# Two batches of the first modulation at a time, from batch 12 on

## The chip, the cores and the metric

The kernel runs on one core of one Trainium2 chip. The metric is the device time of one execution in microseconds, as the median of the runs shown. The engines are named as the profile names them: PE is TensorE's matmul side, PEld its weight loads, DVE is VectorE, ACT is ScalarE, POOL is GpSimd and SP is SyncE, which here does nothing but issue loads and stores. "POOLq" and "SPq" are the two queues from which transfers are issued.

## What is computed

A two-layer backbone over 512 tokens and 256 context tokens, both 2048 wide, in float32. Only its start matters here:

```
shift, scale, gate       = split(silu(c) @ w_mod + b_mod, 3)        # w_mod: 2048 x 6144, layer 0
shift_c, scale_c, gate_c = split(silu(c_ctx) @ w_mod + b_mod, 3)
h  = rmsnorm(x,   g) * (1 + scale)   + shift       # 512 x 2048
hc = rmsnorm(ctx, g) * (1 + scale_c) + shift_c     # 256 x 2048
q, k, v, f, z = split(h @ w_in)                    # the first product made is k, and kc from hc
```

Windowed attention, a Fourier mixing, an output projection, a second layer with pooling and a last norm follow. The second layer's modulation and the gate of the first are made on DVE beside the later stages.

## The kernel before

All large products are made in three parts of reduced precision (high by high, high by low, low by high), so a value is first split into a high and a low part: ACT makes the high part (`w_hi`, `h_hi`, `hc_hi`), DVE the low one (`w_lo`, `h_lo`, `hc_lo`). A "unit" is one pair of 128-row tiles of the contraction, 0.5 MB of weights; a projection stage for 512 output columns has 8 units (HALVES), each used by 4 products of output tiles, m = 0 to 3.

The opening stage interleaves two things on PE, in an order written out by hand:

- The first modulation, in 32 batches (BATCHES). Batch k reads two loads of 0.5 MB of `w_mod`, 1 MB together, and issues 16 products with the conditioning vector as the stationary operand (the trace counts each product as two instructions). Batches 4p to 4p+3 add up to shift and scale of the pair of tiles p. After its last product a batch raises `mod_used`.
- The key projection of tokens and of context. A **key chunk** is one unit by one output tile over 512 tokens, 6 matmuls of 512 columns; a **context chunk** is the same over 256 context tokens. There are 32 of each. Chunks 4u to 4u+3 belong to unit u and need the normed, split pair u, which needs batches 4u to 4u+3.

`KEY_STEPS` and `CONTEXT_STEPS` say which chunks follow which batch: at step k PE runs `modulate(k)`, then the step's key chunks, then its context chunks; steps 32 and 33 have no batch. `opening_steps(start, counts, steady, total)` turns a list of counts from step `start` on, and `steady` after it, into ranges; step 32 is always filled up to chunk 27 and step 33 holds the last four.

The queues around it:

- **SP** loads the batches. There are three slots (BATCH_SLOTS) of 1 MB: two in `raw`, one in `modchunk`. `load_batch(k)` (L358) waits until batch k-3 is used. After batch 31, SP loads weights of the next stage into the same slots (L352).
- **POOL** issues the key weights one unit at a time into the single buffer `key_raw`: unit u+1 is issued (L396) when DVE has made the low part of unit u. Behind unit 7 it issues `cond_row` (1 MB), `rope` (0.5 MB) and `edges` (L401 to L403), which the stages after the opening need.
- **ACT** makes for each pair u the high part of the key weights (`hi(G_K, u)`, L437), which waits until PE has finished the context chunks of unit u-2, and after it the high parts of `h` and `hc` (L461).
- **DVE** turns the modulation of pair u (L953 to L958, once batch 4u+3 is used), norms the two tiles (L863), makes `w_lo` (L798), then `h_lo` (L872), then the context pair.

After the opening comes the value stage: its first unit (`w_lo` from `raw`) is split on ACT and DVE behind pair 7 and behind the conditioning row (L520, L996). From there on the stages are paced by PE.

Of the kernel before, what the change touches and what calls it, by code (L numbers as in the profile page):

```python
# [29 lines left out]
GROUP = 4  # L30
QUADRANT = P // 4
COLS = GROUP * P
HALVES = KT // 2
# [107 lines left out]
def opening_steps(start, counts, steady, total):  # L141

    at, steps = 0, []
    for k in range(BATCHES + 2):
        n = counts[k - start] if 0 <= k - start < len(counts) else steady * (k >= start)
        end = {BATCHES: total - GROUP, BATCHES + 1: total}.get(k, at + n)
        steps.append(range(at, end))
        at = end
    return steps


KEY_STEPS = opening_steps(3, (2, 1, 1, 0, 0, 1, 1, 1, 1, 0, 1, 1, 1, 1, 0, 1, 1, 1, 1, 1, 1, 0), 1, GROUP * HALVES)
CONTEXT_STEPS = opening_steps(7, (4, 0, 0, 2, 2, 0, 0, 0, 0), 1, GROUP * HALVES)
SUM_X_STEP, SUM_C_STEP = 1, 5
AWAKE_STEP, AWAKE_PRODUCTS = 3, 5
CONTEXT_SLOTS = 4
# [19 lines left out]
def build(nc, mod0, weights, modb, cond_in, xT, ctxT, vectors, wf, ident_in, identb_in, masks_in, rope_in, dft_tok_in,  # L176
          dft_ch_in, edges_in, outT):
    with ExitStack() as whole:
# [1204 lines left out]
        def _(pe):  # L1383
# [121 lines left out]
            pe.wait_ge(cond_ready, 1)  # L1505
            for k, (key_part, context_part) in enumerate(zip(KEY_STEPS, CONTEXT_STEPS)):
                if k < BATCHES:
# [367 lines left out]
```

## Time and profile before

| | us |
|---|---|
| median of 3 runs | 1447.12 |
| lowest and highest | 1446.72, 1449.27 |
| the profiled execution | 1448.78 |
| its span, first to last instruction | 1447.1 |
| PE busy in it | 1413.7 (98%) |
| DVE, ACT, POOL busy | 904.9, 501.2, 77.1 |
| PE in the chain that ended last | 88% |

Times in the trace are counted from the span's start. A duration of a matmul is longer than the distance to the next one, since matmuls overlap; for PE the distance between starts is what counts. The opening takes the first 137 us of the span.

### The profile page before, as it was taken

The page shows a single profiled execution, that of the slowest core. Times are in us where ns is not written, and L with a number is a line of the kernel's source. Part 1 is how long each engine was busy: PE and PEld are TensorE (multiplying, and loading weights), DVE is VectorE, ACT ScalarE, POOL GpSimd, SP SyncE. Part 2 cuts the span into 40 slices and gives each one's busy share as a digit, 9 for nine tenths or more (in the row PEclk, how much of TensorE's full clock was granted, in tenths as well). Part 3 has the DMA queues.
Part 4 walks back from the last instruction along what each step waited for, and adds up shares of the span by engine and source line. Part 5 has one row for each costly group of instructions (what it writes and reads, how often), then busy time and mean ns, then how long its engine had stood idle before and what let it go on. Part 6 is the DMA issues. An engine that isn't in the chain of part 4 may idle for free.

```text
span 1447.1 us, 20122 instructions
## 1 busy us (share of the span) xinstructions
PE 1413.7 (98%) x7714; PEld 1182.7 (82%) x7714; DVE 904.9 (63%) x1422; ACT 501.2 (35%) x730; POOL 77.1 (5%) x148
## 2 busy tenths in 40 slices
PE   5899999999999999999999999999999999999997
PEld 3688888888888888888888888888888888888897
DVE  6644555546767787776565676664555666674456
ACT  5223322234555443354222342121351323332233
POOL 0001111101100000000001101000000000010000
PEclk9999999999999999999999999999999999999998
DMA  9996567556711333324666666333233233366344
GB/s 385 379 378 248 175 204 251 176 174 201 230 58 58 103 117 116 111 78 145 203 191 196 195 190 190 117 101 102 88 102 98 92 97 93 93 203 187 105 144 172
DMA packets 65099, 236.87 MB, mean 164 GB/s; under 512 B 7232, under 2 KB 8128, under 8 KB 63744
## 3 DMA queue, kind: packets, MB, share of 16 engines
q1 hardware_dynamic: 43344, 157.83, 32.6%
q0 software_dynamic: 19712, 72.03, 15.7%
q10 hardware_dynamic: 1968, 5.95, 1.2%
q8 instruction: 54, 0.88, 0.3%
q14 instruction: 21, 0.17, 0.0%
HBM read 231.59 MB, written 4.19 MB: 163 GB/s over the span
## 4 chain that ended last, share of the span: by engine, by line
PE 88%; DMA 5%; DVE 5%; issue 1%; ACT 1%; SPq 0%; DVEq 0%; POOLq 0%; POOL 0%; ACTq 0%
PE ps L1385 86%; DMA modchunk<-in_modb 2%; DMA raw<-in_mod 2%; PE ps L1613 2%; DMA kvmem<-in_ctxT 1%; DVE modchunk L805 1%; DVE w_lo L798 1%; DVE stat L1065 0%; DVE pooled L1346 0%; DVE tmp L917 0%; DVE kvmem L981 0%; DVE pt_lo L1104 0%; DVE main L921 0%; ACT w_hi L437 0%; DVE tmp L1076 0%
## 5 line engine op out<-in xcount | busy, mean ns | idle before, releaser
L1385 PE MATMUL ps<-h_hi,w_hi 128*128 128x512 f32 (+1 forms) x1664 | 643.9, 387 | 2.7 <-DVE h_lo L872 1.3
L1385 PE MATMUL ps<-h_hi,w_lo 128*128 128x512 f32 (+1 forms) x1664 | 634.6, 381 | 0.0
L1385 PE MATMUL ps<-h_lo,w_hi 128*128 128x512 f32 (+1 forms) x1664 | 634.3, 381 | 0.0
L798 DVE TENSOR_TENSOR w_lo<-raw,w_hi 128x1024 fp32r<-128x1024 f32 x216 | 264.4, 1224 | 359.3 <-ACT w_hi L437 359.0
L437 ACT CAST w_hi<-raw 128x1024 fp32r<-128x1024 f32 x216 | 226.6, 1049 | 649.2 <-PE ps L1385 649.1
L1385 PEld LDWEIGHTS ps<-h_hi,w_hi 128*128 128x128 f32 x1664 | 312.9, 188 | 66.1 <-issue 7.7
L1385 PEld LDWEIGHTS ps<-h_hi,w_lo 128*128 128x128 f32 x1664 | 312.8, 188 | 61.3
L1385 PEld LDWEIGHTS ps<-h_lo,w_hi 128*128 128x128 f32 x1664 | 313.1, 188 | 57.0 <-issue 0.2
L805 DVE CUSTOM_DVE_ANT_0 modchunk<-modchunk,cond_row 128x1024 f32<-128x1024 f32 x128 | 154.7, 1220 | 20.3 <-DMA modchunk<-in_modb 20.1
L392 POOL DMA_DIRECT2D modchunk<-in_modb x128 | 67.6, 528 | 1143.3 <-DVE modacc L805 1117.5
L641 ACT CAST pt_hi<-ps 128x512 fp32r<-128x512 f32 (+1 forms) x48 | 30.7, 640 | 124.0 <-PE ps L1613 124.0
L1065 DVE TENSOR_REDUCE stat<-ps 128x1 f32<-128x513 f32 (+1 forms) x48 | 36.3, 757 | 38.2 <-PE ps L1385 38.2
L1244 DVE SCALAR_TENSOR_TENSOR ubuf<-raw,modv,ubuf 128x512 f32<-128x512 f32 x60 | 45.0, 749 | 2.3 <-DVE ubuf L1266 1.2
L1385 PE MATMUL ps<-raw,kvmem 128*32 128x128 f32 x704 | 26.1, 289 | 17.7 <-DMA raw<-in_mod 17.6
L1385 PEld LDWEIGHTS ps<-raw,kvmem 128*32 128x32 f32 x704 | 18.8, 114 | 23.6 <-issue 17.5
L1104 DVE TENSOR_TENSOR pt_lo<-ps,pt_hi 128x512 fp32r<-128x512 f32 (+1 forms) x48 | 36.1, 753 | 2.6 <-ACT pt_hi L641 2.4
L1385 PE MATMUL ps<-k_hi,q_hi 128*128 128x256 f32 (+1 forms) x96 | 32.5, 339 | 0.2 <-DVE q_lo L1046 0.2
L1385 PE MATMUL ps<-k_lo,q_hi 128*128 128x256 f32 (+1 forms) x96 | 28.4, 296 | 0.0
L1385 PE MATMUL ps<-k_hi,q_lo 128*128 128x256 f32 (+1 forms) x96 | 28.2, 294 | 0.0
L1385 PE MATMUL ps<-p_hi,w_hi 128*128 128x512 f32 x64 | 25.2, 394 | 0.0
L1385 PE MATMUL ps<-p_hi,w_lo 128*128 128x512 f32 x64 | 25.1, 392 | 0.0
L1385 PE MATMUL ps<-w_hi,h_lo 128*128 128x512 f32 x64 | 25.0, 390 | 0.0
(204 smaller groups left out, 1332.1 us busy)
## 6 DMA issues: line engine op xcount, KB each, us to landing
raw<-in_weights SPq DMA_DIRECT2D x216, 512.0 KB, 3.6
modchunk<-in_modb POOLq DMA_DIRECT2D x128, 512.0 KB, 4.6
raw<-in_mod SPq DMA_DIRECT2D x44, 512.0 KB, 6.8
modchunk<-in_mod SPq DMA_DIRECT2D x20, 512.0 KB, 6.9
main<-in_xT SPq DMA_DIRECT2D x4, 1024.0 KB, 8.3
main<-in_xT ACTq DMA_DIRECT2D x4, 1024.0 KB, 4.9
out<-pooled SPq DMA_DIRECT2D x14, 256.0 KB, 2.1
kvmem<-in_weights POOLq DMA_DIRECT2D x6, 512.0 KB, 7.1
```

The source lines that it names most:

```text
L392: pool.dma_start(modchunk[:, slot], src).then_inc(chunk_landed[slot], 16)
L437: nc.scalar.copy(w_hi[:, j % 2], src).then_inc(hi_ready, 1)
L641: nc.scalar.copy(*turned_tiles(k - 1, pt_hi)).then_inc(pt_hi_ready, 1)
L798: nc.vector.tensor_tensor(w_lo[:, j % 2], src, w_hi[:, j % 2].bitcast(F32), ALU.subtract).then_inc(lo_ready, 1)
L805: nc.vector.tensor_tensor_reduce(out=modchunk[:, half], in0=modchunk[:, half], in1=cond_row[:, half * (D // 2):(half + 1) * (D // 2)], sca ...
L1065: chain.link(nc.vector.tensor_reduce(stat[:, 0, par:par + 1], ps_flat[:, S_END - width:S_END], AX.X, ALU.max))
L1104: nc.vector.tensor_tensor(lo_part, turned_part, hi_part.bitcast(F32), ALU.subtract).then_inc(pt_ready, 1)
L1244: ins = nc.vector.scalar_tensor_tensor(out=bias_acc[g % 2], in0=raw[:, j % RAW_SLOTS, r], scalar=shift, in1=bias_acc[g % 2], op0=ALU.mult, ...
L1385: return nc.tensor.matmul(out, lhsT, rhs, start=start, stop=stop, skip_group_check=True)
L1613: ins = nc.tensor.transpose(ps_flat[:, 6 * 512 + t * P:6 * 512 + (t + 1) * P], probs[k % 2][:, t * P:(t + 1) * P], ident)
```

## The change

From batch 12 on PE takes two batches one after the other and then two key chunks and two context chunks, in place of one batch, one key chunk and one context chunk. The slots, the loads and what they wait for stay as they are.

```
-KEY_STEPS = opening_steps(3, (2, 1, 1, 0, 0, 1, 1, 1, 1, 0, 1, 1, 1, 1, 0, 1, 1, 1, 1, 1, 1, 0), 1, GROUP * HALVES)
-CONTEXT_STEPS = opening_steps(7, (4, 0, 0, 2, 2, 0, 0, 0, 0), 1, GROUP * HALVES)
+KEY_STEPS = opening_steps(3, (2, 1, 1, 0, 0, 1, 1, 1, 1) + (0, 2) * 10, 0, GROUP * HALVES)
+CONTEXT_STEPS = opening_steps(7, (4, 0, 0, 0, 2) + (0, 2) * 10, 0, GROUP * HALVES)
```

Worked out into chunks (key / context) after each batch:

| step | before | after |
|---|---|---|
| 10 | 1 / 2 | 1 / 0 |
| 11 | 1 / 2 | 1 / 2 |
| 12 | none | none |
| 13 | 1 / 0 | 2 / 2 |
| 14, 15 | 1 / 0, 1 / 0 | none, 2 / 2 |
| 16, 17 | 1 / 1, 0 / 1 | none, 2 / 2 |
| 18 to 23 | 1 / 1 each | none and 2 / 2 in turn |
| 24 | 0 / 1 | none |
| 25 | 1 / 1 | 2 / 2 |
| 26 to 31 | 1 / 1 each | none and 2 / 2 in turn |
| 32 | 3 / 4 | 0 / 2 |
| 33 | 4 / 4 | 4 / 4 |

Steps 0 to 9 are the same in both.

## Rows read from the trace of the kernel before

**Rows 1.** Windows: length, busy time (instructions) by engine, granted clock, DMA share, GB/s.
```profile
66.00:72.00 6.00, 4.16 (x71) 2.58 (x70) 3.66 (x8) 2.43 (x3) 0.10 (x1) 1.00 1.02 414
...
96.00:102.00 6.00, 6.00 (x93) 4.95 (x91) 4.66 (x9) 3.19 (x5) 0.53 (x1) 1.00 0.97 350
```

**Rows 2.** Waits of PE from 60 to 119.6: total us, times, longest.
```profile
PE ps L1385 <- DMA raw<-in_mod: 2.2, 4, 0.7
```

**Rows 3.** Chain that ended last: start us, length, what.
```profile
68.60 8.75 DMA raw<-in_mod
...
77.39 82.67 PE ps L1385 x784
```

**Rows 4.** Timeline of PE in the opening: start us, length, instruction, count, idle before.
```profile
54.58 0.28 PE L1385 MATMUL ps<-hc_hi,w_hi 128*128 128x256 f32 x1
...
60.10 1.96 PE L1385 MATMUL ps<-raw,kvmem 128*32 128x128 f32 x64
62.08 0.47 PE L1385 MATMUL ps<-h_hi,w_hi 128*128 128x512 f32 x1
...
74.48 1.08 PE L1385 MATMUL ps<-modchunk,kvmem 128*32 128x128 f32 x32
75.50 0.39 PE L1385 MATMUL ps<-hc_hi,w_hi 128*128 128x256 f32 x1
```

**Rows 5.** The same, around the last batches and up to the value stage.
```profile
117.70 0.28 PE L1385 MATMUL ps<-hc_hi,w_hi 128*128 128x256 f32 x1
...
118.50 1.08 PE L1385 MATMUL ps<-raw,kvmem 128*32 128x128 f32 x32
119.51 0.50 PE L1385 MATMUL ps<-h_hi,w_hi 128*128 128x512 f32 x1
...
121.00 0.28 PE L1385 MATMUL ps<-hc_hi,w_hi 128*128 128x256 f32 x1
...
121.71 0.39 PE L1385 MATMUL ps<-h_hi,w_hi 128*128 128x512 f32 x1
...
125.82 0.28 PE L1385 MATMUL ps<-hc_hi,w_hi 128*128 128x256 f32 x1
...
128.65 0.40 PE L1385 MATMUL ps<-h_hi,w_hi 128*128 128x512 f32 x1
...
136.95 0.40 PE L1385 MATMUL ps<-w_hi,h_hi 128*128 128x512 f32 x1
```

**Rows 6.** Batch loads issued 64.7-65.4 (batch 17), 99.7-100.4 (28), 109.7-110.4 (31), then 77.9-110.5.
```profile
L358 SPq DMA_DIRECT2D modchunk<-in_mod x2: 328/436/545, 64.8 to 65.1; - x2
DMA to landing us min/median/max: 8.1/8.5/9.0
...
DMA to landing us min/median/max: 7.5/7.9/8.3
...
DMA to landing us min/median/max: 5.1/5.9/6.6
...
DMA to landing us min/median/max: 4.2/6.2/8.3
```

**Rows 7.** Timeline of POOL from 111 to 113.5.
```profile
111.35 0.53 POOL L396 DMA_DIRECT2D kvmem<-in_weights  x1 [11.28 <-DVE w_lo L798]
111.86 0.53 POOL L401 DMA_DIRECT2D cond_row<-in_cond  x1
```

**Rows 8.** Timeline of DVE and of ACT: pair 3, then pair 7 and the first value unit.
```profile
68.23 0.32 DVE L953 STREAM_TRANSPOSE kvmem<-ps 128x128 f32<-128x128 f32 x1 [4.45 <-PE ps L1385]
...
71.52 1.41 DVE L872 SCALAR_TENSOR_TENSOR h_lo<-main,mod_v,h_hi 128x512 fp32r<-128x512 f32 x2
...
121.96 1.05 ACT L437 CAST w_hi<-kvmem 128x1024 fp32r<-128x1024 f32 x1 [8.25 <-PE ps L1385]
...
124.19 1.41 DVE L872 SCALAR_TENSOR_TENSOR h_lo<-main,mod_v,h_hi 128x512 fp32r<-128x512 f32 x2
...
132.84 1.22 DVE L798 TENSOR_TENSOR w_lo<-raw,w_hi 128x1024 fp32r<-128x1024 f32 x1
```

## The prediction

> **What bounds the kernel now.** I went from the whole to the part. In the chain that ended last PE has 88% and the one long piece that is not PE in this region ends at 77.4 us; from there the chain is PE's own work [rows 3]. So whatever shortens PE's sequence in the opening after 77.4 should move the end, if no wait takes its place. The waits of PE say what else is in the opening: from batch 12 on it waits 2.2 us in four places, each time for a batch's load [rows 2]. The windows explain why these waits stop: between 66 and 72 us the transfers run at 414 GB/s with PE at 4.16 of 6.00 us, so the loads set the pace; between 96 and 102 they run at 350 GB/s with PE busy throughout, so PE does, with some 15% of the transfer rate in hand [rows 1]. The granted clock is 1.00 in all of these windows, so no term of the sum comes from it.
>
> Then the distances between starts. A single batch takes 1.01 (118.50 to 119.51), the first key chunk behind it 1.49 (to 121.00), a context chunk behind that 0.71 (to 121.71), a key chunk behind a chunk 1.37 (three in 4.11, to 125.82), a context chunk in front of a batch 0.80 (117.70 starts the last one, 118.50 the batch) [rows 5]. Two batches in a row take 1.98 (60.10 to 62.08) [rows 4].
>
> **The change part by part.**
>
> *Fewer changes of kind.* Two steps of before cost 2 x (1.01 + 1.49 + 0.80) = 6.60. One pair of after costs 1.98 + 1.49 + 1.37 + 0.71 + 0.80 = 6.35. In steady steps that is 0.25 a pair; counted by kind, a change costs 0.12 (1.49 against 1.37) plus 0.09 (0.80 against 0.71) plus 0.04 (2.02 against 1.98), again 0.25. No product is added or dropped. From step 17 to 31 before has 15 groups of chunks behind a batch and after has 8: 7 x 0.25 = 1.75 us less. (Groups before step 17 don't count, since the loads set the pace there.)
>
> The Trainium skill ("TensorE: Matmul & The Clock Gate", Back-to-back issue gap) gives the distance of matmuls as set by the number of columns and the pipelined weight load, and knows no price for a change of kind. By that this term would be zero; the trace disagrees, with 1.49 against 1.37 for the same six products [rows 5].
>
> *Order up to batch 17.* Step 10 loses its two context chunks (1.4 us, from 54.58 on) [rows 4], so batch 13 ends between 60.7 and the 62.08 of now [rows 4], by how much of this its loads leave. Two groups of chunks at 4.37 and two pairs of batches at 1.98 later, at 73.4 to 74.8, batch 17 would be done by PE's own order. But the last half of its load is issued at 65.1 now and lands 9.0 later, at 74.1 [rows 6]; a rate that is full already won't bring it sooner. A batch needs half of its 1.01 after its second load, so batch 17 ends at 74.6, against 75.50 now [rows 4]: 0.9 gained. Bounds: 1.0, and nothing, since after issues this load two microseconds later than now (batch 14 waits for four chunks more), at about 67.2, and by the 8.3 of batch 28 it would land at 75.5.
>
> *What is behind it.* From 75.50 to the first chunk of unit 7 at 128.65 are 53.15 us [rows 4, 5]. Of these goes the last of the four waits (0.3, one of those in rows 2, the one that ends at 77.39 [rows 3]), the 1.75 for changes of kind, and one context chunk (0.71), which after has made by batch 17 (chunks 8 and 9 at step 15, where before had made chunk 8 alone by then). Remaining: 50.4. So unit 7 could start at 125.0 but for new waits: 3.65 gained.
>
> *New wait for loads.* With three slots batch k+3 is issued when batch k ends. The first batch of a pair then has nearly two pairs of time, the second has one: its second half is issued 0.5 after batch k and is wanted one pair, 6.35 us, after its own issue. Now it has three steps of 3.3 less a batch, 8.9. The latencies seen from 78 us on are 4.2 to 8.3, median 6.2 [rows 6]; so the cover is thin. But much of these is standing in line: in after nothing has been issued for 5.3 us when the second of a pair is, and the four loads of a pair take 4 x 1.27 = 5.1 at 414 GB/s [rows 1]. The line is empty, and I take the smallest latencies seen, 4.2, and 0.9 more for a second half, which is issued 0.4 behind the first and takes 1.27, so 5.1 [rows 6], plus 1.3 where POOL's key load of 0.5 MB shares the engines: 6.4 at most. No wait in the pairs 18/19 to 28/29; bounds 0 and 2.0, which is four pairs that meet a key load, each late by a quarter of the 2.0 by which batch 28's 8.3 would miss.
>
> Batch 31 is another matter. Its load goes out when batch 28 ends, at about 111.7. POOL issues the weights of unit 7 and behind them 1.5 MB for later stages when `w_lo` of unit 6 is made: at 111.35 and 111.86 now [rows 7], about 110.4 then. So 2 MB of POOL's and 1 MB of SP's are in flight together. If the two queues share evenly, batch 31 has its 4 halves' worth to wait for, two of its own and two of POOL's: 5.1 + 2 x 1.27 = 7.6, that is 1.3 late. Before, batch 31 with half of this overlap took 6.6 (0.3 late), and batch 28, issued right beside a key load, 8.3 (2.0 late) [rows 6]. I take 0.8; bounds 0 and 2.0.
>
> The Trainium skill ("DMA: Bandwidth & Descriptors", Queues, rings and completion order) says that each DMA engine takes turns between the queues it has work for, a packet at a time. By that rule it would be the even share, 1.3, and the result 0.5 worse than my sum; strict order of issue would give 3.0 or more. No row of before separates the two, since there the two queues overlap for a part of a batch only.
>
> *New wait for the splits.* Now unit 7's `h_lo` is made 6.1 us after batch 31 ends (119.51 to 125.6), because ACT's `w_hi` waits for PE's context chunks (idle 8.25 before it, until PE) [rows 8]. In after those chunks, of unit 5, are done two steps earlier, so the cast is off the chain, as for pair 3, where it took 68.1 to 72.93, 4.8 us [rows 8]. PE has between batch 31 and unit 7 two key and four context chunks: 1.49 + 1.37 + 4 x 0.71 = 5.7. So 5.7 against 4.8: no wait, 0.9 in hand. Were the cast still late, it would cost 0.4. The same holds for units 3 to 6 with 4.37 + 1.98 = 6.35 between.
>
> *The value stage.* It starts at 136.95, behind unit 7's 8.30 us, and its first `w_lo` is ready at 134.06 [rows 5, 8], 14.55 after batch 31 ended. The latter chain begins with pair 7, so it gets 1.1 shorter: 13.4 after batch 31, which ends at 74.6 + 7 x 6.35 + 0.8 = 119.85, thus 133.3. PE reaches unit 7 at 119.85 + 5.7 = 125.55 by this count, at 125.8 by the one above, and the value stage 8.3 later, at 133.85 to 134.1. Covered by at least 0.5; nothing lost. The loads of modb start when batch 31 is used, as before; the later stages are paced by PE, so the shift carries to the end.
>
> **Sum:** 0.9 + 0.3 + 1.75 + 0.7 - 0.8 = 2.85 us less. The profiled execution took 1448.78 with its span of 1447.1 us; it would become 1445.9. It lies 1.7 above the median of the runs, which is what is forecast: 1447.12 - 2.85 = 1444.3.
>
> **The rivals.**
>
> A. *The second batch of each pair is late* (slower). Place: PE in front of batches 19, 21 ... 29, with the slots full. Price: latency of a second half minus 6.35, in each of six pairs. It decides from 6.35 + 2.85/6 = 6.8 on; at the even-share 7.6 in all pairs it would cost 6 x 1.25 = 7.5, so 1444.3 + 7.5 = 1452. For it: the median of all latencies is already 6.2. Against: nothing else is in line when it is issued, and rates have room [rows 1]. Chance 0.09.
>
> B. *Late only beside POOL's key loads*, by the bound of 2.0 in all: 2.85 - 2.0 = 0.85 gained, 1446.3; if batch 31 is 2.0 late as well, 1447.5. For it the 8.3 of batch 28. Chance 0.27.
>
> C. *The change of kind costs the same somewhere else*, as the page has it: the 1.75 is not there: 1446.05. Chance 0.08.
>
> D. *Batch 31 is on time.* POOL's packets start late enough: 0.8 more, and the value stage just meets its weights: 1443.5. Chance 0.18.
>
> Forecast (1443.9 to 1445.0): 0.38.
>
> **How the numbers follow.** What a measurement here can tell from no change is 0.2%, 2.9 us, so faster means under 1444.2. D is, and half of the forecast's case: 0.45 with a little for unknown gains. A is the slower side, over 1450.0; with mishaps not named, 0.10. The rest, B and C and the other half of the forecast, 0.45, is within. For the range: D, less the 0.25 between the two counts and the 0.4 by which the fastest run of before lies under the median, gives 1442.8; upwards B with both its parts is 1447.5. A is left out.
>
> **What would show it.** The wait of 0.3 at 77.4 and those before it are smaller in sum; pairs of batches repeat every 6.35 us; batch 17 ends near 74.6 and batch 31 near 119.9 with a wait of about 0.8 in it; unit 7 starts near 125.8 and the value stage near 134.1, both without a wait for DVE. A wait before the second batch of every pair would be A; pairs of 6.6 us without waits would be C. The forecast is wrong if the value stage starts later than 136 or the gain there is not found at the end of the span.

## The result and the profile after

| | before | after |
|---|---|---|
| median us (11 runs each) | 1448.38 | 1453.43 |
| range | 1446.72 to 1452.50 | 1449.29 to 1455.91 |
| profiled execution, span | 1447.1 | 1454.2 |
| value stage starts (span's clock) | 136.95 | 145.17 |

The ratio is 1.003, with a 95% interval of 1.0021 to 1.0039. The forecast was 2.85 us less, 1444.3, counted from 1447.12, the median of the first three runs, which lies 1.3 under that of all eleven. By the ratio it became some 4.3 us more (0.3% of 1448; the two medians lie 5.05 apart), outside the range of 1442.8 to 1447.5. The profiled execution of after took 1455.91 in all and is the slowest of its eleven, so its terms below are somewhat larger than those of a median run.

The page of after. PE is as busy as before, 1413.8 against 1413.7, over a longer span. No product was added. That the busy time is equal does not show that nothing slowed: the two key chunks at half the clock, below, add 1.8 us to it. Three per cent of the chain that ended last are loads of `in_mod` into `raw`.

```profile
span 1454.2 us, 20122 instructions
PE 1413.8 (97%) x7714; PEld 1184.1 (81%) x7714; DVE 904.3 (62%) x1422; ACT 501.7 (34%) x730; POOL 77.1 (5%) x148
PE ps L1385 88%; DMA raw<-in_mod 3%; PE ps L1613 2%; DMA kvmem<-in_ctxT 1%; DVE w_lo L798 1%; DMA modchunk<-in_mod 1%; DVE stat L1065 0%; DVE pooled L1346 0%; DVE tmp L917 0%; DVE kvmem L981 0%; DVE pt_lo L1104 0%; DVE modchunk L805 0%; DVE main L921 0%; SPq L358 0%; DVE tmp L1076 0%
```

Windows of after (length; busy time and instructions of PE, PEld, DVE, ACT, POOL; granted clock; DMA share; GB/s), against [rows 1]. PE now waits between 96 and 102 too, where it was busy throughout; the granted clock is 0.58 from 126 to 129, 0.50 from 129 to 133 (half of full speed, 1.2 in place of 2.4 GHz) and back at 1.00 in the course of the microsecond after that. Read one microsecond at a time it is 0.73 from 126 to 127 and 0.50 from 127 to 133, so it stood at half from 126.5 to 133.3, 6.8 us. PE had waited 3.3 us up to 125.82 and worked 0.65 when it fell.

```profile
96.00:102.00 6.00, 5.76 (x72) 4.93 (x76) 4.94 (x11) 1.39 (x2) 0.53 (x1) 1.00 0.95 330
121.00:126.00 5.00, 1.73 (x45) 1.33 (x47) 0.00 (x0) 1.04 (x1) 0.00 (x0) 1.00 1.01 405
126.00:129.00 3.00, 1.08 (x28) 0.78 (x24) 0.00 (x0) 0.00 (x0) 0.00 (x0) 0.58 0.78 315
129.00:133.00 4.00, 4.00 (x21) 2.85 (x12) 3.36 (x8) 1.38 (x2) 0.00 (x0) 0.50 0.58 203
```

The waits of PE from 50 to 130 (total, times, longest), against [rows 2], and the loads in the chain of after (start, length, what), against [rows 3]. Before had one such load after 61 us in its chain besides the one in [rows 3], and none behind 77.4; after has them up to 128.

```profile
PE ps L1385 <- DMA raw<-in_mod: 8.0, 6, 3.3
PE ps L1385 <- DMA modchunk<-in_mod: 1.5, 2, 1.1
```

```profile
61.65 7.55 DMA raw<-in_mod
...
75.69 7.36 DMA raw<-in_mod
...
95.82 8.08 DMA raw<-in_mod
...
116.73 11.62 DMA raw<-in_mod
...
128.39 17.64 PE ps L1385 x103
```

The timeline of PE around batch 31, against [rows 5]. The first row is batch 30, the next two are the halves of batch 31, each behind a wait for its load. Then the key chunks: the distance between matmuls is 0.43 us (130.42 to 130.85) until 133, and 0.22 to 0.23 again from 133.36 on. Six of them take 1.37 at the full clock; the two key chunks take 4.65 (129.40 to 134.05) in place of 2.86.

```profile
121.47 1.08 PE L1385 MATMUL ps<-raw,kvmem 128*32 128x128 f32 x32
125.82 0.65 PE L1385 MATMUL ps<-raw,kvmem 128*32 128x128 f32 x16 [3.27 <-DMA raw<-in_mod]
128.39 1.08 PE L1385 MATMUL ps<-raw,kvmem 128*32 128x128 f32 x16 [1.92 <-DMA raw<-in_mod]
129.40 0.80 PE L1385 MATMUL ps<-h_hi,w_hi 128*128 128x512 f32 x1
...
130.42 0.63 PE L1385 MATMUL ps<-h_hi,w_lo 128*128 128x512 f32 x1
130.85 0.63 PE L1385 MATMUL ps<-h_hi,w_hi 128*128 128x512 f32 x1
...
133.36 0.39 PE L1385 MATMUL ps<-h_hi,w_hi 128*128 128x512 f32 x1
```

What stood beside batch 31's load: POOL's timeline, against [rows 7], and the two loads of batch 31 issued at 116.3 and 116.7, against [rows 6]. POOL issued its 2 MB (unit 7, `cond_row`, `rope`) from 114.64 on, 1.7 us ahead of batch 31; before it issued them 1.2 us behind it.

```profile
114.64 0.53 POOL L396 DMA_DIRECT2D kvmem<-in_weights  x1 [13.50 <-DVE w_lo L798]
115.16 0.53 POOL L401 DMA_DIRECT2D cond_row<-in_cond  x1
```

```profile
L358 SPq DMA_DIRECT2D raw<-in_mod x2: 328/376/424, 116.3 to 116.7; - x2
DMA to landing us min/median/max: 9.4/10.5/11.6
```

The queues in the stretch from 118 to 121 and then from 121 to 126 (packets, MB, share of the 16 engines); q0 is POOL's, q1 SP's. For three microseconds SP's queue moves 0.05 MB and POOL's 0.99; then they go about evenly by packets (294 and 227) and by bytes. The first packet of batch 31 comes at 120.10, 3.8 us after the load was issued; the load issued at 129.53, with hardly anything else in flight, has its first packet 1.0 us later.

```profile
q0 software_dynamic: 181, 0.99, 89.5%
q1 hardware_dynamic: 12, 0.05, 6.3%
...
q1 hardware_dynamic: 294, 1.09, 54.8%
q0 software_dynamic: 227, 0.94, 46.3%
```

The kernel before has the same thing, where nothing waits for it. There SP issues the first weights of the value stage at 116.33 and 116.70, 5.0 us behind POOL's first transfer; their first packet comes at 119.47, and they land after 7.3 and 8.3 us. From 116.3 to 119.4 the view has no row for SP's queue; POOL's:

```profile
q0 software_dynamic: 218, 1.23, 97.6%
```

The splits of pair 7 on DVE, against [rows 8]: the transpose begins at 129.53, `h_lo` is done at 134.22, 4.8 us behind the batch's end at 129.40. PE comes to unit 7 at 136.87. That part went as forecast.

```profile
129.53 0.32 DVE L953 STREAM_TRANSPOSE kvmem<-ps 128x128 f32<-128x128 f32 x1 [12.00 <-PE ps L1385]
...
132.82 1.40 DVE L872 SCALAR_TENSOR_TENSOR h_lo<-main,mod_v,h_hi 128x512 fp32r<-128x512 f32 x2
```

### The profile page after: what moved, and what is told of

Its sections match the earlier page's. It is cut to its first block, busy times and chain, and to the rows that moved or that the text cites. A ratio compares the mean times of both kernels' runs of the same rounds, so it can differ in the third digit from the quotient of the medians.

```text
span 1454.2 us, 20122 instructions
## 1 busy us (share of the span) xinstructions
PE 1413.8 (97%) x7714; PEld 1184.1 (81%) x7714; DVE 904.3 (62%) x1422; ACT 501.7 (34%) x730; POOL 77.1 (5%) x148
## 4 chain that ended last, share of the span: by engine, by line
PE 89%; DMA 5%; DVE 4%; issue 1%; ACT 1%; SPq 0%; DVEq 0%; ACTq 0%
PE ps L1385 88%; DMA raw<-in_mod 3%; PE ps L1613 2%; DMA kvmem<-in_ctxT 1%; DVE w_lo L798 1%; DMA modchunk<-in_mod 1%; DVE stat L1065 0%; DVE pooled L1346 0%; DVE tmp L917 0%; DVE kvmem L981 0%; DVE pt_lo L1104 0%; DVE modchunk L805 0%; DVE main L921 0%; SPq L358 0%; DVE tmp L1076 0%
```

## The experiments

Theory 1: PE reaches batch 31 behind a burst of 2 MB on POOL's queue, waits, and then pays a second time in clock. Theory 2: with three slots the second batch of a pair has too short a lead (6.3 us in place of 8.9) whatever else is in flight. They are compatible; the question was what each costs. "Filler" is products whose result nobody uses; a wait is idle time of PE of over 0.15 us. "Value stage" is the start of that stage in the profiled execution: the timeline's first matmul on `ps<-w_hi,h_hi`.

| kernel | median us | ratio to before (95%) | value stage | waits of PE for batches 11 to 31 |
|---|---|---|---|---|
| before | 1448.2 to 1448.8 | 1 | 136.95 | 2.2 |
| after | 1453.43 | 1.0030 (1.0021 to 1.0039) | 145.17 | 9.5 |
| e1 POOL late | 1451.04 | 1.0016 (1.0007 to 1.0025) | 138.81 | 5.9 |
| e2 four slots | 1442.26 | 0.9957 (0.9943 to 0.9970) | 131.01 | 0 |
| e3 filler | 1451.40 | 1.0022 (1.0013 to 1.0031) | 138.71 | 3.0 and 2.8 of filler |
| e4 singles at the end | 1451.68 | 1.0019 (1.0009 to 1.0029) | 142.06 | 6.5 |
| c2 before, four slots | 1445.09 | 0.9974 (0.9964 to 0.9985) | 134.73 | 0 |
| e5 before, half loads | 1445.31 | 0.9980 (0.9970 to 0.9990) | 134.16 | 0 |
| e6 after, half loads | 1445.27 | 0.9974 (0.9965 to 0.9984) | 134.15 | 2.1 |
| e8 before, short lead | 1463.01 | 1.0097 (1.0082 to 1.0113) | 152.96 | 11.6 |
| c1 before, POOL late | 1448.93 | 1.0001 (0.9991 to 1.0012) | 139.70 | 2.5 |
| e9 = e1 + e4 | 1448.61 | 0.9997 (0.9988 to 1.0005) | 138.41 | 3.4 |
| after again | 1455.57 | 1.0041 (1.0027 to 1.0055) | 144.59 | 8.7 |

**e1, POOL's late loads held back** (on top of after):

```
+            pool.wait_ge(mod_used, BATCHES - 2)
             pool.dma_start(cond_row[:], cond_in).then_inc(cond_row_landed, 16)
```

> After, with one more wait: POOL issues cond_row, rope and edges only when batch 29 is used. Theory 1 (the burst of 2 MB on POOL's queue makes the last batch late; 5.2 us of waits and then 6.8 us at half the clock): the wait in batch 31 falls from 5.2 to under 1.5 us, the clock stays at full, the value stage starts some 6 us earlier (139 instead of 145), and the time is 1447 to 1449, near before. Theory 2 (three slots are too few for pairs, whatever POOL does): batch 31 still waits 3 us or more and the time stays at 1451 to 1453.

The key weights of unit 7 still go out ahead of batch 31's load; what is held back is 1.5 MB. The wait in batch 31 fell from 5.2 to 2.1 us and the clock stayed at 1.00; the value stage starts 6.4 us earlier. The row is PE's waits from 118 to 130 in e1.

```profile
PE ps L1386 <- DMA raw<-in_mod: 2.1, 1, 2.1
```

The median fell by 2.4 only, less than theory 1 gave (4 to 6), and 1451.04 lies in what theory 2 gave (1451 to 1453). In this profile 2.65 us come back as one wait for `w_lo` at 247.7, in the stage after the value stage, where before waits 0.7 and after not at all. So theory 1 holds in its mechanism (the wait, the clock, the value stage) and not in its time; theory 2 holds too, since 2.1 us of waiting remained in batch 31 and 3.8 in the batches ahead of it.

**e2, a fourth slot** of 1 MB in `cond_row`, which is not needed before the opening ends (on top of after; the lines for the new slot's semaphores are left out here, and what stands in brackets is shortened). It also holds back POOL's late loads, until batch 28 is used, as e1 does until batch 29, so against e1 it prices the slot, and against after the slot and the burst together:

```
-BATCH_SLOTS = 3
+BATCH_SLOTS = 4
-        mod_units = [raw[:, j] for j in range(RAW_SLOTS)] + [...modchunk...]
+        mod_units = [cond_row[:, j * (D // 2):(j + 1) * (D // 2)]... for j in range(2)] + [
+            raw[:, j] for j in range(RAW_SLOTS)] + [...modchunk...]
+            pool.wait_ge(mod_used, BATCHES - 3)
             pool.dma_start(cond_row[:], cond_in).then_inc(cond_row_landed, 16)
```

> After, with a fourth slot of 1 MB in cond_row's place, whose own load then follows batch 28. A load is issued one batch earlier and the second batch of a pair has two batches and a group more to land. Theory 2 (the lead of a load under three slots is the cause of the waits in batches 15 to 25, 3.5 us together): these waits go to under 0.5 us, batch 31 is on time as well, the pairs run at 6.25 us, and the time is 1443.5 to 1445.5, under before. Rival (the rate of the transfers is the bound, not the lead): waits of 2 us or more stay in batches 13 to 25 and the time is that of e1 or above.

No wait of PE is left from 50 to 136, the pairs repeat every 6.26 us (85.67 to 91.93), and the time is 6.0 us under before, a little better than expected. Its value stage starts 7.8 us earlier than in e1 (131.01 and 138.81). Its timeline of PE, one pair, the start of batch 30 and the start of the value stage:

```profile
85.67 0.50 PE L1388 MATMUL ps<-h_hi,w_hi 128*128 128x512 f32 x1
...
90.05 1.08 PE L1388 MATMUL ps<-raw,kvmem 128*32 128x128 f32 x32
90.94 1.06 PE L1388 MATMUL ps<-modchunk,kvmem 128*32 128x128 f32 x32
...
91.93 0.50 PE L1388 MATMUL ps<-h_hi,w_hi 128*128 128x512 f32 x1
...
115.11 1.08 PE L1388 MATMUL ps<-raw,kvmem 128*32 128x128 f32 x32
...
131.01 0.40 PE L1388 MATMUL ps<-w_hi,h_hi 128*128 128x512 f32 x1
```

The loads did not become quicker. From 60 to 108 they take 4.9 to 10.0 us, median 7.3, where after has 4.0 to 9.6, median 6.7 (62 to 114); they are only asked for earlier:

```profile
DMA to landing us min/median/max: 4.9/7.3/10.0
```

And the rate was there: from 60 to 119.3 e2 moves 385 GB/s with PE at 59.28 of 59.30 us.

```profile
60.00:119.30 59.30, 59.28 (x826) 51.02 (x819) 29.33 (x64) 15.89 (x24) 3.75 (x8) 1.00 0.99 385
```

After moves 346 GB/s in this stretch. So the lead, and not the rate, held PE up in after.

**e3, filler in front of batch 31** (on top of after):

```
+                if k == BATCHES - 1:
+                    pe.wait_ge(mod0_ready, PAIRS - 1)
+                    for _ in range(3):
+                        mm(ps[:, ROW_BANKS[0]], ones, cond_cols..., True, True)
```

> After, with 3 filler products of 512 columns on PE in front of batch 31, in the time in which it waits for its load (3.3 us); POOL and slots as in after. If the fall of the clock to 0.5 behind that wait is a cost of its own (0.5 us in the second half of batch 31 and 1.8 us in the two key chunks), the clock stays at 1.00 or falls for less, the wait before batch 31 turns into filler, and the time is 1.5 to 2.5 us under after, about 1451. If the clock is no cost of its own (what it slows is hidden behind the splits of unit 7), the time stays at that of after, 1453.

The filler (first row) fills the time until the load; 0.54 us of waiting are left, and the clock is 1.00 in the windows in which after had 0.58 and 0.50. The median is 2.0 us under after, as expected of a clock that costs by itself, but the two intervals overlap (1.0013 to 1.0031, and 1.0021 to 1.0039), so the times alone would not carry it; the distances of the matmuls at either clock do. The value stage comes 6.5 us earlier than in after, of which the clock's part (2.3 by the prices of after) is a third. The rest is no merit of the filler: the waits ahead of batch 31 were smaller in this execution, and batch 31's load, issued 1.7 us behind POOL's as in after, landed after 8.4 and 9.7 us in place of 9.4 and 11.6.

```profile
120.17 2.84 PE L1385 MATMUL ps<-kvmem,ones_r 128*128 128x512 f32 x6
122.95 0.64 PE L1385 MATMUL ps<-raw,kvmem 128*32 128x128 f32 x16
124.13 0.64 PE L1385 MATMUL ps<-raw,kvmem 128*32 128x128 f32 x16 [0.54 <-DMA raw<-in_mod]
```

```profile
126.00:129.00 3.00, 3.00 (x21) 2.70 (x20) 3.00 (x5) 1.39 (x2) 0.50 (x1) 1.00 0.90 329
```

**e4, pairs up to batch 27 and single steps behind** (on top of after):

```
-... (0, 2) * 10, 0, GROUP * HALVES)
+... (0, 2) * 8 + (1,) * 4, 0, GROUP * HALVES)
```

> Pairs up to batch 27, then one batch, one key and one context chunk at a time as before, loads and POOL as in after. Batch 31's load then has 8.9 us of cover instead of 6.3. Theory 1 with its latency of 11.6 us: the wait falls from 5.2 to about 2.5 us and is too short for the clock to fall, so the time is 4 to 5 us under after, 1448.5 to 1449.5. If the waits of the pairs before it are what counts (theory 2), it gains under 2 us: 1451.5 or more.

The wait in batch 31 is 2.5 us (0.60 and 1.88), as expected of a latency of 11.5 against a lead of 8.9. But the clock fell all the same, in the course of the second wait, and stood at half for 3.4 us; the median gained 1.8 and not 4 to 5, with intervals that overlap. That expectation was missed: I had taken these waits as too short to bring the clock down.

**c2, the fourth slot in before**, the same edit as e2.

> Before (one batch, one key and one context chunk at a time), with the fourth slot in cond_row's place and nothing else changed. It tells what of e2's 6 us belongs to the slot and what to the pairs. If the pairs give the 9 x 0.25 us of fewer changes of kind once the loads are on time, this kernel loses the 2.2 us of waits of before and no more: value stage at 134.5 to 135, time 1445.5 to 1446.5, some 3 us above e2. If the slot alone does it, it equals e2: 1442 to 1443.

Time as expected or a little better, 1445.09, and no wait of PE from 50 to 136. The value stage starts 2.2 us earlier than in before. That this equals the 2.2 us of waits in [rows 2] is chance: batch 11 starts at 56.73 in c2 and at 56.09 in before, so c2 made up 2.9 us from there on. The idle time of a wait is less than what the wait costs, by some 0.2 us each (the sum of the shift, in the next part, shows it). From c2 to e2 it is 3.7 us more. The first key chunk behind batch 11 comes 2.05 us later in c2 than in e2 (57.74 and 55.69), of which 1.42 are the two context chunks that e2 has put off and 0.63 an earlier start; 3.1 us remain for nine groups of chunks fewer behind a batch (19 and 10 from batch 12 on), 0.34 each. In the medians, each against its own runs of before, the gains are 6.0 and 3.7, 2.3 apart.

**e5 and e6, loads of half the size from batch 12 on** in before and in after (the other half of each slot keeps what was in it, so neither makes the right modulation; they are for timing only):

```
+                    n = COLS if k >= 3 * GROUP else 2 * COLS
```

> Before, with the loads of batches 12 to 31 cut to half their size (the other half of each slot keeps what was in it, so the modulation is computed from wrong weights). With the loads out of the way PE's own order is left: no wait for a load from batch 16 on, value stage at 134.5 to 135.

> After, with the same halved loads from batch 12 on (modulation from wrong weights as well). Against e5 it prices the order alone: nine changes of kind fewer at 0.25 us make it 2.3 us earlier, value stage at 132 to 132.8, no waits in batches 15 to 31, and the clock stays at full. If the order has no gain of its own, both start the value stage at the same time to 0.5 us.

e5 as expected. e6 missed: the value stage starts at 134.15, the same as e5. Its timeline shows that batch 31 waits even for halved loads. They were issued at 111.01 and 111.39, 1.7 us behind POOL's 2 MB, which are not halved, and landed after 7.5 and 8.2 us, where the halved loads have a median of 4.3 to 4.7. That the burst is the reason is read from this and was not tried by itself. With these waits and one of 0.44 in batch 11 taken off it would be 132.0, the expected place.

```profile
118.51 0.64 PE L1386 MATMUL ps<-raw,kvmem 128*32 128x128 f32 x16 [1.29 <-DMA raw<-in_mod]
119.58 0.64 PE L1386 MATMUL ps<-raw,kvmem 128*32 128x128 f32 x16 [0.43 <-DMA raw<-in_mod]
```

**e8, before with a short lead**, loads of batches 15 to 31 issued one batch later:

```
-                    sp.wait_ge(mod_used, k + 1 - BATCH_SLOTS)
+                    sp.wait_ge(mod_used, k + 1 - BATCH_SLOTS + (k >= 15))
```

> Before, but from batch 15 on SP issues a load one batch later than the slots would allow, so that every load has two steps of 3.3 us less a batch, about 5.6 us, in place of 8.9; order of PE, POOL and slots as before. If the lead of a load decides and not the order on PE, waits of about 1 us appear in front of most batches, 10 to 18 us in all: 1458 to 1466. If the rate of transfers or POOL's burst is the cause, there is little change: under 1452.

1463.0, inside the range expected of the lead alone, with before's order on PE. The waits of PE are 11.6 us in 13 places, and the clock falls twice. Of the waits 4.1 us are in batch 31, whose load here goes out 2.9 us behind POOL's burst, so that part is not the lead's alone.

```profile
PE ps L1385 <- DMA raw<-in_mod: 10.8, 11, 2.8
PE ps L1385 <- DMA modchunk<-in_mod: 0.8, 2, 0.6
```

**c1, before with POOL's late loads held back**, the edit of e1.

> Before, with POOL's cond_row, rope and edges issued only when batch 29 is used: the control for e1. In before they go out 1.0 us ahead of that point and after the last batch's load, so if their cost in after comes from being ahead of that load, nothing changes here: 1447.5 to 1449, within 1 us of before. If POOL's burst costs something by itself (the splits, the weights of the value stage), this gains or loses over 1 us.

No difference, 1.0001. POOL's burst costs nothing where it comes behind batch 31's load. (In its profiled execution batch 15 waited 1.9 us and the clock fell 0.6 us behind that wait, so its value stage is late; the execution, 1449.96, is 1.0 over its median.)

**e9, e1 and e4 together** on top of after.

> Pairs up to batch 27, single steps from 28 on (as e4), and POOL's late loads held until batch 29 is used (as e1): what is left of after without its end. If the end of the opening (burst, short lead of batch 31, clock) and the pairs' own waits are separate terms, batch 31 waits under 0.5 us, the waits of batches 13 to 27 stay at 2.5 to 3.5 us, the value stage starts at 137 to 138 and the time is 1448 to 1449.5: no better than before, with the gain of fewer changes of kind eaten by these waits. If the end was all, it is under before by 2 us or more (1446.5).

The same time as before, as expected. Batch 31 no longer waits. PE's waits from 50 to 136 in e9:

```profile
PE ps L1386 <- DMA raw<-in_mod: 2.1, 4, 0.6
PE ps L1386 <- DMA modchunk<-in_mod: 1.3, 3, 0.6
PE ps L1386 <- DVE h_lo L873: 1.2, 1, 1.2
```

3.4 us for loads in batches 11 to 27, and 1.2 us for `h_lo` at 130.03, in front of unit 7, which I had not counted: single steps leave one key and three context chunks behind batch 31, 1.49 + 3 x 0.71 = 3.6 us, for splits that take 4.8.

**After once more**, unchanged.

> The changed kernel once more, on the chip of c1 and e9, to have a second profile: waits of 2.5 to 4 us in batches 11 to 27 and of 4 to 5.5 us in batch 31, with the clock at half behind it. If the drop of the clock was particular to the first profile, it is missing here and the time of this execution is about 2 us nearer to before.

The same picture, so neither the wait nor the clock was particular to one execution: 4.5 us in batch 31, whose halves landed after 9.1 and 10.9 us, 4.2 before it, and half the clock from 126.3 on for 6.8 us.

```profile
126.00:129.00 3.00, 1.62 (x18) 1.10 (x19) 0.44 (x2) 0.00 (x0) 0.00 (x0) 0.56 0.76 300
```

## Why the prediction was wrong

*Fewer changes of kind: right in kind, too small.* Priced at 0.25 us and counted seven times, they are worth 0.34 (c2 against e2), nine times once no load holds the first pairs up. A pair takes 6.26 and not 6.35: two batches in a row take 1.88 (90.05 to 91.93), and I had read 1.98 off one place [rows 4]. Rival C, that there is no such price, is refuted, and with it what the Trainium skill ("TensorE: Matmul & The Clock Gate", Back-to-back issue gap) would make of this term.

*Order up to batch 17: the step failed.* Batch 17 should end at 74.6 and ends at 76.06. The load of batch 17 landed at 74.62, close to the 74.1 assumed, but batches 11 to 15 had waited 2.0 us in four places for theirs (1.09, 0.13, 0.15, 0.61), so PE's own order was behind and not, as I had it, just level. The 1.4 us that step 10 loses went into the wait of batch 11 (1.09 idle; 2.31 from its start to the next chunk in place of 1.01), since its load did not come earlier.

*New wait for loads, the pairs: the step failed.* It said that "the line is empty" when the load of a second batch is issued, because nothing had been issued for 5.3 us. It was not: batch 18's second half was issued at 70.32 and landed at 77.13, 1.8 us after batch 19's load went out at 75.32. The second halves of batches 19 to 29, the second of each pair, took 7.4, 6.2, 6.6, 8.1, 7.5 and 4.8 us, and not the 5.1 to 6.4 of the prediction; only for batch 29 was the line empty. All loads from 62 to 114 took 4.0 to 9.6 us with a median of 6.7. The lead was 6.3, and somewhat more where a wait had drawn the pair out. I had worked out the point from which this rival decides (6.8 us) and put 0.09 on it, though the median of [rows 6] was 6.2 and that of the second halves alone, which are the ones to wait for, 6.7. The bill was 0.93 in batch 19, 0.42 in batch 23 and 1.25 in batch 25, in all 2.6 us of idle time behind batch 17, where the sum had 0.

*Batch 31: the step failed by the most.* Taken 0.8, bounds 0 and 2.0; measured 5.2, and 4.5 the second time. Two errors. The issue order: POOL's three transfers went out 1.7 us ahead of batch 31's load, where in before they follow it by 1.2. I had seen this (110.4 against 111.7) but priced it by rows in which they went out behind it. And the sharing: SP's queue got next to nothing for three microseconds, so the 2 MB were ahead for the most part, and batch 31 landed after 9.4 and 11.6 us, not 7.6. The prediction says that no row of before separates an even share from the order of issue. One does: the weights of the value stage issued at 116.33, behind the same burst, without a packet until 119.47.

The Trainium skill ("DMA: Bandwidth & Descriptors", Queues, rings and completion order) has the engines taking turns between queues at packet granularity. The trace agrees from 121 on (294 and 227 packets). The 12 against 181 from 118 to 121 do not refute it: the section counts 9 to 17 descriptors to a packet, and if each moves 4 KB, as most of the profile's packets do, one turn of one queue on all 16 engines is 0.6 to 1.1 MB, by an estimate from that figure. POOL's 0.99 MB are within it. What failed is my reading of the rule as an even share from the first microsecond; that the turns are this long is not shown by any run.

*The clock: a term that was missing.* The prediction took the granted clock of 1.00 for settled because [rows 1] show it. It held there, with waits of 0.7 us at most. Behind the 3.3 us wait of batch 31 it fell to half for 6.8 us, which costs 0.5 in the second half of batch 31 (1.01 from 128.39 to 129.40, in place of 0.5) and 1.8 in the two key chunks. With filler in that place (e3) it stayed at 1.00.

*The splits and the value stage: right.* 4.8 us behind the batch, no wait. The `w_lo` of the value stage is ready at 142.7, 13.3 behind batch 31 (13.4 forecast), and PE comes at 145.17.

*The sum of the shift.* The value stage starts 8.2 us later in the profiled executions. The terms are counted from start to start, each against the same step of c2 or e2, which have no wait. This is more than the idle time, by some 0.2 to 0.3 us a wait. Batch 11 of after shows it: 2.31 us from 54.83 to 57.14 in place of 1.01, with 1.09 of them idle. Its first half is 0.65 us long, where without a wait the second half would start 0.5 behind the first: what overlaps otherwise stands in line here.

```profile
54.83 0.65 PE L1385 MATMUL ps<-modchunk,kvmem 128*32 128x128 f32 x16
56.56 0.65 PE L1385 MATMUL ps<-modchunk,kvmem 128*32 128x128 f32 x16 [1.09 <-DMA modchunk<-in_mod]
57.14 0.50 PE L1385 MATMUL ps<-h_hi,w_hi 128*128 128x512 f32 x1
```

| term | us |
|---|---|
| waits of before gone (idle 2.2) | -2.9 |
| nine changes of kind | -3.1 |
| waits in batches 11 to 27 (idle 4.3) | +6.2 |
| batch 31 (idle 5.2), without the clock | +5.5 |
| half the clock, 0.5 and 1.8 | +2.3 |
| other starts of the opening in these executions | +0.2 |
| together | 8.2 |

The third term is what batches 30 and 31 start late against e2 (121.47 and 115.11, 6.36) less the 0.15 by which batch 11 starts later; the fourth is 7.93 from there to the next chunk, in place of 1.88, less the clock's 0.5.

*Carried to the end: mostly.* Of 8.2 us at the value stage 7.1 are there at the end of the span; e1, e2 and c2 lose 2.2, 2.4 and 0.8 us more behind the value stage than before does, for the most part through a wait for `w_lo` around 242 to 255 that is between 0 and 2.7 us long from one execution to the next. In e2 that wait is 1.9 us, and the clock falls to half behind it for 3.4 us (0.83 in the mean from 245 to 255); this profiled execution is also the slowest of e2's five (1445.26). It does not follow how early the opening ended (e5, with 134.16, has none), and what sets it was not tried.

## What to carry to other kernels

A load's lead is the time from the slot's release to its use, for each load and not on average: doing work in twos leaves the mean as it is and takes 2.6 of 8.9 us off the lead of every second load. Compare it with the upper half of the latencies in the trace, not the lowest, and count the queue from all issuers, in order of issue, at the moment in question. When an order of work that saves PE time is wanted, give it the slots first: here the pairs, worth 3.1 us by themselves at the value stage, came out 4.3 us behind the kernel before with three slots and 6.0 us ahead of it with four, where the slot alone brings 3.7. And a wait costs more than its idle time: 0.2 to 0.3 us at each of them here, and 2.3 us where the clock fell behind it.

## What had not been expected of the hardware

- The granted clock fell to 0.50 around waits of a few microseconds: for 6.8 us behind a wait of 3.3 us (with one of 1.9 following), for 3.4 us in e4 in the course of a wait of 1.9 us, with 0.6 us of work between it and one of 0.6, for 6.8 us in c1 behind one of 1.9, and for 3.4 us in e2 behind one of 1.9 us. In e1 waits of 2.1 and of 2.65 us left it at 1.00, so the length of the last wait alone does not tell. At half the clock the matmuls of 512 columns lie 0.43 us apart in place of 0.23.
- Transfers of 0.5 MB issued on SP's queue 1.7 us behind 2 MB on POOL's moved almost nothing for three microseconds (0.05 MB against 0.99), and landed after 9.4 and 11.6 us. In after's second execution and in e3 they moved 0.20 and 0.15 MB in such a stretch, against 1.06 and 1.04, and landed after 9.1 and 10.9, and 8.4 and 9.7 us. Behind no such burst the same loads take 4.0 to 9.6 in after.
- Two batches of small products in a row take 1.88 us and one alone 1.01. An order with nine groups of chunks fewer between batches is 0.34 us faster for each: a change between products with 32 stationary columns and those with 128 has a price, there and back. The kernels compared here don't part this price by product.
- A wait of PE costs some 0.2 us more than its idle time (2.31 us in place of 1.01, with 1.09 idle).
